# The order of blocks in a gated-linear-attention stage: both directions, with waits on states by block

## What is computed

```python
def gla_chunked(q, k, v, log_a):      # chunks of 64 tokens, n = T // 64
    ...
    q_in = q * jnp.exp(b); k_in = k * jnp.exp(-b); k_end = k * jnp.exp(b_last - b)
    o_intra = (lower triangle of q_in k_in^T) v
    u = k_end^T v                      # one 64 x 128 sum for each chunk
    def step(s, inp):                  # state: s -> decay * s + u, chunk after chunk
        d_c, u_c = inp
        return d_c[..., None] * s + u_c, s
    ...
    return o_intra + q_in s_prev
o = gla_chunked(q, k, v, la_f) + flip(gla_chunked(flip(q), flip(k), flip(v), flip(la_b)))
o = o * rsqrt(mean(o * o) + eps) * norm_g * silu(g)      # for each token and head
```

## Time and profile before

| | |
|---|---|
| median of 3 runs | 3385.62 us |
| the profiled execution's own time | 3386.37 us |
| its span, first to last instruction | 3384.1 us |
| TensorE busy | 3177.5 us, 94% |
| VectorE busy | 1744.9 us, 52% |
| ScalarE busy | 1105.5 us, 33% |
| mean granted TensorE clock | 0.971 |
| first stage, to the first matmul of `natten` | 0 to 791.7 us |
| of it pass 0 | to 188.5 us |

### The profile page before, as it was taken

The page is one execution under the profiler, slowest core; times in us unless marked ns, Lnnn a source line. Parts: engine busy times, 40 slices in busy tenths (PEclk is TensorE's granted clock), DMA queues, the critical chain, the costliest instruction groups (busy, mean ns, idle before and its releaser), DMA issues.

```text
span 3384.1 us, 42316 instructions
## 1 busy us (share of the span) xinstructions
PE 3177.5 (94%) x15664; PEld 2548.7 (75%) x15664; DVE 1744.9 (52%) x3389; ACT 1105.5 (33%) x2118; POOL 372.8 (11%) x374
## 2 busy tenths in 40 slices
PE   6998998885999995999999999999999999999997
PEld 4776766664777774788888888888888888888885
DVE  6647646742666663555645335353353533543377
ACT  2346245421443441444333222132222222222222
POOL 0012100004333400000003000030000200020000
PEclk9999999987999998899999999999999999999998
DMA  7799697848777738788787556575565755656553
GB/s 265 298 301 277 232 289 243 285 150 240 252 227 254 252 141 324 282 308 290 254 317 288 199 188 235 198 287 197 190 234 197 289 195 193 233 202 236 193 197 114
DMA packets 267883, 807.95 MB, mean 239 GB/s; under 512 B 44706, under 2 KB 111138, under 8 KB 220320
## 3 DMA queue, kind: packets, MB, share of 16 engines
q1 hardware_dynamic: 234784, 608.11, 52.6%
q10 hardware_dynamic: 21312, 155.20, 12.8%
q0 software_dynamic: 11584, 41.95, 3.3%
HBM read 622.04 MB, written 187.24 MB: 239 GB/s over the span
## 4 chain that ended last, share of the span: by engine, by line
PE 58%; DVE 2%; DMA 2%; ACT 0%; issue 0%; SPq 0%; POOL 0%; DVEq 0%; ACTq 0%
PE trunk_ps_h L76 12%; PE trunk_ps_h L77 12%; PE trunk_ps_h L78 12%; PE trunk_ps_f L76 7%; PE trunk_ps_f L78 7%; PE trunk_ps_f L77 7%; DMA trunk_raw<-in_w_out 1%; DMA trunk_raw<-in_w_down 1%; PE trunk_ps_h L2016 0%; DVE trunk_w L1758 0%; DVE trunk_y L1777 0%; DVE trunk_stats L1781 0%; ACT trunk_w L1675 0%; DVE trunk_y L1814 0%; DVE trunk_y L1816 0%
## 5 line engine op out<-in xcount | busy, mean ns | idle before, releaser
L76 PE MATMUL trunk_ps_h<-trunk_xt,trunk_w 128*128 128x512 f32 x1760 | 685.7, 390 | 1.4 <-DVE trunk_xt L1822 1.4
L77 PE MATMUL trunk_ps_h<-trunk_xt,trunk_w 128*128 128x512 f32 x1760 | 685.4, 389 | 0.0
L78 PE MATMUL trunk_ps_h<-trunk_xt,trunk_w 128*128 128x512 f32 x1760 | 685.4, 389 | 0.0
L1852 DVE SCALAR_TENSOR_TENSOR trunk_tt<-trunk_hb,trunk_cw,trunk_tt 128x512 f32<-128x512 f32 x220 | 187.0, 850 | 678.2 <-ACT trunk_tt L1701 678.2
L76 PE MATMUL trunk_ps_f<-trunk_w,trunk_m 128*128 128x512 f32 x1168 | 456.9, 391 | 20.6 <-DMA trunk_m<-mix_lo 19.3
L78 PE MATMUL trunk_ps_f<-trunk_w,trunk_m 128*128 128x512 f32 x1168 | 455.1, 390 | 0.0
L77 PE MATMUL trunk_ps_f<-trunk_w,trunk_m 128*128 128x512 f32 x1168 | 455.0, 390 | 0.0
L1699 ACT ACTIVATE trunk_hb<-trunk_ps_h 128x512 f32<-128x512 f32 x220 | 131.7, 599 | 885.9 <-PE trunk_ps_h L78 885.9
L76 PEld LDWEIGHTS trunk_ps_h<-trunk_xt,trunk_w 128*128 128x128 f32 x1760 | 330.9, 188 | 70.7 <-DVE trunk_xt L1822 1.8
L78 PEld LDWEIGHTS trunk_ps_h<-trunk_xt,trunk_w 128*128 128x128 f32 x1760 | 330.8, 188 | 68.9
L77 PEld LDWEIGHTS trunk_ps_h<-trunk_xt,trunk_w 128*128 128x128 f32 x1760 | 330.9, 188 | 68.5
(11 more groups left out here) (204 smaller groups left out, 4472.5 us busy)
## 6 DMA issues: line engine op xcount, KB each, us to landing
trunk_w<-wu_s SPq DMA_DIRECT2D x88, 1024.0 KB, 4.8
trunk_w<-wu_s ACTq DMA_DIRECT2D x88, 1024.0 KB, 4.8
near_xr<-xt_s SPq DMA_DIRECT2D x160, 512.0 KB, 5.8
front_xr<-xt_s SPq DMA_DIRECT2D x120, 512.0 KB, 6.3
wu_s<-trunk_w SPq DMA_DIRECT2D x44, 1024.0 KB, 4.8
trunk_w<-wd_s SPq DMA_DIRECT2D x44, 1024.0 KB, 4.8
trunk_w<-wd_s ACTq DMA_DIRECT2D x44, 1024.0 KB, 4.8
trunk_raw<-in_w_up SPq DMA_DIRECT2D x44, 512.0 KB, 5.8
```

The lines of the kernel that those rows point to most:

```text
L76: pe.matmul(out, lh, rh, start=first, stop=False, skip_group_check=skip)
L77: pe.matmul(out, lh, rl, start=False, stop=False, skip_group_check=skip)
L78: return pe.matmul(out, ll, rh, start=False, stop=last, skip_group_check=skip)
L1852: dve.scalar_tensor_tensor(out, hb[:, i, s, a_j:a_j + BLK], tap[:, a_j:a_j + 1], out, ALU.mult, ALU.add).then_inc(conv_step, 1)
```

## The change

Heads 0 and 1 take their inputs from block 0 up and their outputs from block 4 down; heads 2 and 3 the other way round. The third pass (v and g of heads 2 and 3) runs from block 4 down too. Each block's outputs wait for the updates that lead to that block, and the updates of the second chain are spread between the outputs. The inputs of heads 2 and 3 wait by block for the outputs of heads 0 and 1. Each head has its own two update semaphores. All steps of both tables are set anew: the last output begins at step 157 instead of 172, so that 168 steps are run instead of 183. `load_out` moves to s-1 where outputs are three steps apart, `out_hi`, `out_lo` and `store_mix` come one step earlier.

```diff
@@ -122,9 +122,13 @@
 SEQS = ((0, T_PROMPT // CHUNK), (T_PROMPT // CHUNK, NCHUNK))
 CPB = BLK // CHUNK
-IN_AT = {0: [45, 53, 61, 69, 77], 1: [49, 57, 65, 73, 81], 2: [109, 113, 117, 121, 125], 3: [129, 133, 137, 141, 145]}
-OUT_AT = {0: [96, 99, 102, 105, 108], 1: [112, 116, 120, 124, 128], 2: [144, 148, 152, 155, 158],
-          3: [160, 163, 166, 169, 172]}
+UP_BLOCKS, DOWN_BLOCKS = tuple(range(NBLK)), tuple(range(NBLK - 1, -1, -1))
+IN_BLOCKS = (UP_BLOCKS, UP_BLOCKS, DOWN_BLOCKS, DOWN_BLOCKS)
+OUT_BLOCKS = (DOWN_BLOCKS, DOWN_BLOCKS, UP_BLOCKS, UP_BLOCKS)
+PASS_BLOCKS = (UP_BLOCKS, UP_BLOCKS, DOWN_BLOCKS, UP_BLOCKS)
+IN_AT = {0: [46, 61, 65, 69, 77], 1: [53, 57, 73, 81, 85], 2: [91, 96, 112, 115, 118], 3: [109, 125, 128, 131, 134]}
+OUT_AT = {0: [88, 92, 95, 99, 104], 1: [107, 110, 113, 119, 122], 2: [129, 132, 135, 138, 142],
+          3: [145, 148, 151, 154, 157]}
 TAIL = 4
@@ -137,11 +141,16 @@
-    ins = sorted(((h, b) for h in range(GLA_H) for b in range(NBLK)), key=lambda hb: IN_AT[hb[0]][hb[1]])
-    outs = [(h, b) for h in range(GLA_H) for b in range(NBLK)]
+    ins = sorted(((h, b) for h in range(GLA_H) for b in range(NBLK)),
+                 key=lambda hb: IN_AT[hb[0]][IN_BLOCKS[hb[0]].index(hb[1])])
+    outs = [(h, b) for h in range(GLA_H) for b in OUT_BLOCKS[h]]
     in_no = {hb: i for i, hb in enumerate(ins)}
-    in_step = [IN_AT[h][b] for h, b in ins]
-    out_step = [OUT_AT[h][b] for h, b in outs]
+    out_no = {hb: j for j, hb in enumerate(outs)}
+    in_step = [IN_AT[h][IN_BLOCKS[h].index(b)] for h, b in ins]
+    out_step = [OUT_AT[h][OUT_BLOCKS[h].index(b)] for h, b in outs]
+    out_load = [max(s - 4, out_step[j - 2] + 5) if j >= 2 else s - 4 for j, s in enumerate(out_step)]
     def at(steps, n):
@@ -159,25 +168,33 @@
     logit_at, turn_at, sum_at = in_step, shifted(in_step, 6), shifted(in_step, 8)
     soft_at, cum_at, exp_at, scale_at, ktok_at, copy_at = (shifted(in_step, k) for k in (1, 2, 3, 4, 7, 9))
     score_at, o_at, back_at = out_step, shifted(out_step, 2), shifted(out_step, 6)
-    mask_at, root_at, norm_at, hi_at, lo_at = (shifted(out_step, k) for k in (1, 3, 4, 7, 8))
+    mask_at, root_at, norm_at, hi_at, lo_at = (shifted(out_step, k) for k in (1, 3, 4, 6, 7))
     fwd = [(c, c + 1) for c0, c1 in SEQS for c in range(c0, c1 - 1)]
-    bwd = [(c, c - 1) for c0, c1 in SEQS for c in range(c1 - 1, c0, -1)]
-    CHAIN = len(fwd)
+    bwd = [(c, c - 1) for c0, c1 in reversed(SEQS) for c in range(c1 - 1, c0, -1)]
+    def early(h):
+        return int(IN_BLOCKS[h] == DOWN_BLOCKS)
     def chain_steps():
         todo = {}
         for h in range(GLA_H):
-            n = 0
-            for b in range(NBLK):
+            d, n = early(h), 0
+            for b in IN_BLOCKS[h]:
                 ready = copy_at[in_no[h, b]] + 1
-                for i in range(sum(CPB * b <= c < CPB * (b + 1) for c, _ in fwd)):
-                    todo.setdefault(ready + i // 2, []).append((h, 0, n))
+                for i in range(sum(CPB * b <= c < CPB * (b + 1) for c, _ in (fwd, bwd)[d])):
+                    todo.setdefault(ready + i // 2, []).append((h, d, n))
                     n += 1
-            start, end = copy_at[in_no[h, NBLK - 1]] + 1, OUT_AT[h][0]
-            for i in range(CHAIN):
-                todo.setdefault(start + i * (end - start) // CHAIN, []).append((h, 1, i))
+            d, n, begin = 1 - d, 0, copy_at[in_no[h, IN_BLOCKS[h][-1]]] + 1
+            for b in OUT_BLOCKS[h]:
+                count = sum(CPB * b <= to < CPB * (b + 1) for _, to in (fwd, bwd)[d])
+                end = out_step[out_no[h, b]] + 1
+                for i in range(count):
+                    todo.setdefault(begin + i * (end - begin) // count, []).append((h, d, n))
+                    n += 1
+                begin = end
         return todo
     updates = chain_steps()
@@ -248,7 +265,7 @@
         k_end_done, k_in_done, q_in_done = st.sem("k_end_done"), st.sem("k_in_done"), st.sem("q_in_done")
         k_turned, k_tok_done, u_done = st.sem("k_turned"), st.sem("k_tok_done"), st.sem("u_done")
         u_fwd, u_bwd = st.sem("u_fwd"), st.sem("u_bwd")
-        fwd_step, bwd_step = ([st.sem(f"{n}_{i}") for i in range(2)] for n in ("fwd_step", "bwd_step"))
+        fwd_step, bwd_step = ([st.sem(f"{n}_{h}") for h in range(GLA_H)] for n in ("fwd_step", "bwd_step"))
         rep_done = st.sem("rep_done")
         kq_stored = [st.sem(f"kq_stored_{i}") for i in range(2)]
         okq_in, ov_in, og_in = ([st.sem(f"{n}_{i}") for i in range(2)] for n in ("okq_in", "ov_in", "og_in"))
@@ -270,9 +287,22 @@
             return blk + sum(i < blk for i in VG_BLOCKS)
-        def chains(h):
-            return (h // 2 + 1) * CHAIN
+        def made(d, b):
+            return 1 + max(n for n, (_, to) in enumerate((fwd, bwd)[d]) if to // CPB == b)
+        def used(d, b):
+            return 1 + max(n for n, (c, _) in enumerate((fwd, bwd)[d]) if c // CPB == b)
+        def outputs_past(eng, h, b):
+            if h >= 2:
+                eng.wait_ge(o_done, out_no[h - 2, max(b - 1, 0)] + 1)
+        def block_of(n):
+            p, k = divmod(n // KC, NBLK)
+            return PASS_BLOCKS[p][k]
         def split_step(m):
@@ -331,10 +361,10 @@
                 if n < 2 * PER_PASS:
                     sp.wait_ge(xt_stored[m % XRING], 16 * (m // XRING + 1))
                 sp.wait_ge(stepped, n - XRING + 1)
-                sp.dma_start(xr[:, n % XRING].bitcast(F32), xt_s[m // KC, m % KC]).then_inc(xt_in[n % XRING], 16)
+                sp.dma_start(xr[:, n % XRING].bitcast(F32), xt_s[block_of(n), n % KC]).then_inc(xt_in[n % XRING], 16)
             def store_out(blk):
-                p, b = divmod(blk, NBLK)
+                p, b = blk // NBLK, block_of(blk * KC)
                 if blk in VG_BLOCKS:
                     pair = slice((p - VG01) * VG_W, (p - VG01 + 1) * VG_W)
                     for u in range(UNITS):
@@ -355,8 +385,9 @@
                 sp.dma_start(dst, src.to_broadcast([PAIRS, QB_C, BIAS_ROWS * RPB_C])).then_inc(rep_done, 16)
             def vg_stored(h, b):
+                p = VG01 + h // 2
                 for u in range(UNITS):
-                    sp.wait_ge(out_stored[u], 16 * stored_by((VG01 + h // 2) * NBLK + b + 1))
+                    sp.wait_ge(out_stored[u], 16 * stored_by(p * NBLK + PASS_BLOCKS[p].index(b) + 1))
             def store_lr(b):
                 sp.wait_ge(lr_copied, b + 1)
@@ -466,9 +497,9 @@
                     load_v(i)
                 for i in at(shifted(in_step, 6), n):
                     store_kq(i)
-                for j in at(shifted(out_step, -4), n):
+                for j in at(out_load, n):
                     load_out(j)
-                for j in at(shifted(out_step, 9), n):
+                for j in at(shifted(out_step, 8), n):
                     store_mix(j)
                 if NV * PER_PASS <= n < NSTEP and n % 2 == 0 and n % PER_PASS < 4 * ROWS_U:
                     copy_bias(*divmod(n % PER_PASS // 2, 2))
@@ -560,9 +591,9 @@
             def decays(i):
                 (h, b), s = ins[i], i % 2
                 act.wait_ge(rest_done, 2 * (i + 1))
-                if b == 0 and h >= 2:
-                    act.wait_ge(bwd_step[h % 2], chains(h - 2))
-                    act.wait_ge(fwd_step[h % 2], chains(h - 2))
+                if h >= 2:
+                    act.wait_ge(bwd_step[h - 2], used(1, b))
+                    act.wait_ge(fwd_step[h - 2], used(0, b))
                 chunks = slice(b * CPB, (b + 1) * CPB)
                 act.activation(z[:, s, :], z[:, s, :], ACT.Exp, scale=1.0 / TAU).then_inc(exp_done, 1)
                 act.activation(decay[0:DK, h % 2, chunks], e[0:DK, s, CHUNK - 1::CHUNK], ACT.Exp,
@@ -582,8 +613,7 @@
             def copy_sums(i):
                 h, b = ins[i]
-                if b == 0 and h >= 2:
-                    act.wait_ge(o_done, (h - 1) * NBLK)
+                outputs_past(act, h, b)
                 if (h, b) == (1, 0):
                     act.wait_ge(state_set, 2 * len(SEQS))
                 for half in range(2):
@@ -726,8 +756,7 @@
             def copy_sums(i):
                 h, b = ins[i]
-                if b == 0 and h >= 2:
-                    dve.wait_ge(o_done, (h - 1) * NBLK)
+                outputs_past(dve, h, b)
                 if (h, b) == (1, 0):
                     dve.wait_ge(state_set, 2 * len(SEQS))
                 for half in range(2):
@@ -741,11 +770,11 @@
             def update(h, d, n):
                 c, to = (fwd, bwd)[d][n]
-                done, sums = ((fwd_step[h % 2], u_fwd), (bwd_step[h % 2], u_bwd))[d]
-                need(dve, done, chains(h) - CHAIN + n)
-                last_in = in_no[h, c // CPB if d == 0 else NBLK - 1]
+                done, sums = ((fwd_step[h], u_fwd), (bwd_step[h], u_bwd))[d]
+                need(dve, done, n)
+                last_in = in_no[h, c // CPB if d == early(h) else IN_BLOCKS[h][-1]]
```

(6 more changed lines are left out.)

## The result

The changed kernel takes 3403.4 us (median of 8 runs, 3394.99 to 3411.11), and 3384.8 us (median of 8) in the same comparison for the kernel before: a ratio of 1.005, 95% interval 1.0039 to 1.0061. It is **slower by half a per cent**, 18.6 us. I had forecast 3369 us, and 3392 as the upper end: the sign was wrong and the range too low.

A forecast was written before the change was run, and what follows sets the result against it. First stage bound by TensorE in dense steps, with VectorE and ScalarE queues sometimes late, and by latency in the tail. Tail -62.1, moved work +33.0, waits +5, clock +7: -17 from 3386.4 gives 3369 us (forecast 3362 to 3377, range 3350 to 3392).

The forecast's parts named there:

- What moves out of the tail: First stage's tail: five scores, six output groups and five turns back move beside dense work, lengthening TensorE's dense part 33.0 us.
- What is left of the tail: Behind the last output's squares: 15.1 us stay before the next stage, so 62.1 of the tail's 77.2 us go.
- The walk's own waits: VectorE's and ScalarE's queues followed through the new tables: 35 us of TensorE waits from step 90 to 142.
- What the new order costs in waits: Packed steps of the first stage: 35 us of waits where steps 85 to 159 had 30, so +5 us.
- The clock, "+7 us": Dense part: two to three more waits that drop matmuls to half clock, 2.9 us each, +7 us.
- Slower: SyncE's queue: Steps 111 to 115: load_w behind a late VectorE split holds SyncE's queue; three such events give 3402 us, chance 0.06.
- Two dense steps and the outputs between, 9.6 us: Lead of load_out at s-1 before the scores: 9.6 us, against 5 to 6 us for a load.
- Waits stay at or below those of before: Rival, first stage: waits stay within 30 us and its clock loss, giving 3357 us, or 3345; chance 0.30.
- The queues become the bound: Rival, steps 107 to 127 and 128 to 142: waits a third longer drag the clock, about 3382 us; chance 0.20.
- Semaphores, the order of blocks in pass 2 and waits by block cost nothing: First stage: no instruction of work added, same load sizes, blocks stored at least a step before their load; 0 us.
- The table's drain: ScalarE table switches: the skill's some 1380 ns drain left out of the sum; with it 5 to 6 us worse, near 3375.

The follow-up runs named there:

- the run with six places: The changed kernel with six places instead of three for raw weights in the first stage, loads at the same steps: way 608.9 us, ratio 1.0009 to the kernel before.
- the old tables: The changed kernel with the previous step tables, load_out at s-4, out_hi, out_lo and store_mix one step later again: way 601.0 us, ratio 0.9987 to the kernel before.

## Why the prediction was wrong

- **"What moves out of the tail" was right.** The dense part's own work grew as said: an output group undisturbed is 4.0 us in the rows above, as in the sum. **"What is left of the tail"** had 19 us from the last dense matmul; it is 18.4. The tail gave its 59 us.
- **The walk's own waits were right in sum.** Found at steps 90, 96, 99, 111 to 117, 126, 131, 136, 139 and 142: 35.2 us. Measured at these: 34.1. Singly they are off by up to 3 us: step 90 6.1 (4.6), 115 0.4 (2.5), 117 7.6 (5.8), 131 4.0 (7), 136 3.4 (5.3).
- **The step that failed is "What the new order costs in waits", +5 us.** I walked VectorE's and ScalarE's queues against TensorE's and compared only the pairs that I thought of: eviction, mask, normalise, update. Some 28 us of waits lay outside of it: the scores of 113 for a load held on SyncE (11.5), outputs of 94, 121, 134 and 137 for the copy of sums, which I had priced on VectorE at 1.3 us but with nobody waiting for it, although chunk sums and outputs share banks of PSUM (3.0, 3.1, 1.2, 3.3), and the scores of 119, 129 and 135 for softplus's first activation, which frees their bank (5.5, the 2.1 of step 129 listed as issue). The rest behind step 84 is below 1.5 us each. So waits rose by 30 us, not 5. The runs agree: taking away the first gave 12 us of way, the second 14 to 17.
- **The clock, "+7 us", was too small.** The dense part grew by 76.4 us. Less 29.6 of waits and the 33 - 4 = 29 of moved work, 18 are left. The granted clock bears this out: it was at half for 44 us of the dense part before and for 89 after (the rounded clocks of the earlier trace rows and of the stretches above give 43 and 88), and of the 45 more at most half is lost. From the starts of the matmuls, those that began at half clock took 18 us more than the usual spacing of their kind before and 35 after. The price of 2.9 us for each time that the clock fell was about right (2.5 to 2.7 by these); the number was not: 7 times before and 13 after, where I had two to three more. It fell with waits that the walk had missed, too, as at steps 94 (3.0 us) and 113 (11.5).
- The account of the way: -59 (tail) + 29 (moved work) + 30 (waits) + 18 (clock) = +18, and 17.5 was measured. The sum closes because the clock's 18 is what the others leave; the two readings above support it.
- **"Slower: SyncE's queue"** had the time right, 3402, by luck: it asked for three events and there was one, of 11.5 us, which the run with six places prices at 12; the other omissions made up for the rest. The sign that I had set for it, a wait for a DMA of over 10 us, did come. I wrote that it decides if the queue is held for longer than the five steps of lead, 14 us, and found 7; it was held for 9.0 and 8.6 us in a row, 18.4 in all. What I left out besides is the pile: stores, gate input, keys and queries, 7 us of issues, went out ahead of the operands that were needed, and these had a shorter lead than dense inputs. "Two dense steps and the outputs between, 9.6 us" was the lead without the pile. A chance of 0.06 for slower was too low, since it took only one such wait beside a few smaller omissions.
- **"Waits stay at or below those of before"** was wrong: the walk was not pessimistic; it was incomplete. **"The queues become the bound"** is wrong as a statement of work: VectorE is busy for 70 of 126 us in the worst stretch, and reordering alone brought it back.
- **"Semaphores, the order of blocks in pass 2 and waits by block cost nothing"**: shown for the old tables, on balance, with a way 2 us under that of before.
- **The table's drain.** Squares behind a softplus, step 116 of the changed kernel, ScalarE:

```profile
532.87 0.63 ACT L587 ACTIVATE front_e<-front_e 128x512 f32<-128x512 f32 x1
533.52 1.28 ACT L589 ACT_TABLE_LOAD   x1
534.82 0.63 ACT L589 ACTIVATE front_e<-front_e 128x512 f32<-128x512 f32 x1
...
536.74 0.23 ACT L631 ACTIVATION_READ_ACCUMULATOR front_region<-front_bank 128x1 f32 x1
536.98 1.28 ACT L636 ACT_TABLE_LOAD   x1
538.28 0.30 ACT L636 ACTIVATE front_rinv<-front_ss,front_rms_eps 128x4 f32<-128x4 f32 x1
```

The load starts 0.02 us or less behind the instruction ahead of it, and the activation 0.02 us behind the load, both times. The Trainium skill (ScalarE: Activation LUTs, "What ACT_TABLE_LOAD costs") adds some 1380 ns of drain to a switch; no gap of that size stands ahead of these loads or behind them, and leaving it out was right. The lost time lay elsewhere.

## What to carry to other kernels

When work is packed closer, make a list of every "A may not start before B" across engines, banks of PSUM that two users share and the DMA-issuing queue included, and walk all of them; the pairs that never waited before are those that appear. In a queue that runs in order, ask of each waiting entry what stands behind it and with how much lead, and put what others wait for ahead of what nobody waits for: two copies moved by one step were worth 15 us. Charge a wait for the half-clocked work behind it as well, and count how often the clock will fall. Judge an edit of a few microseconds by the times of many executions; the profiled one can be the slowest of them.

## What the runs showed of the hardware that I had not expected

A wait of 3.0 us in the midst of dense work was enough for the next group of matmuls to run at half clock (L975 at 0.63 us for 0.39), so that it cost 6 us in all. And 158 us of SyncE standing still kept no dense matmul waiting, where taking away 43 us of it gained 12.
